# One-level Strassen for the query and key projections: seven block products, weight sums on GpSimd, additions on VectorE

## The reference

```python
h = rms_norm(x, pre_norm_gain)            # 256 x 1024
proj = h @ w_in                           # q: 3 x 512 columns, k: 3 x 512 columns, v, rwkv, gates
...
logits = einsum('bdhnqc,bdhnkc->bdhnqk', qb, kb) * scale + bias      # scale = 1 / 8
```

## Time and profile before

| | |
|---|---|
| time, median of 3 runs | 1834.88 us (1834.88 to 1836.4) |
| the profiled execution, own time | 1837.94 us |
| its span, first to last instruction | 1835.8 us |
| PE busy | 1375.2 us (75%) |
| DVE busy | 435.8 us (24%) |
| ACT busy | 144.8 us (8%) |
| POOL busy | 36.4 us (2%), 53 instructions |
| mean granted TensorE clock | 0.855 |
| DMA | 629.55 MB, mean 343 GB/s |

### The profile page before, as it was taken

How to read it: one execution, slowest core, us unless ns; L and a number is a source line. 1 busy time by engine, 2 the same in 40 slices (tenths; PEclk the granted TensorE clock), 3 DMA queues, 4 the chain that set the end, 5 groups by cost and what they waited for, 6 DMA issues and landing times.

```text
span 1835.8 us, 21606 instructions
## 1 busy us (share of the span) xinstructions
PE 1375.2 (75%) x10034; PEld 769.3 (42%) x10034; DVE 435.8 (24%) x671; ACT 144.8 (8%) x316; POOL 36.4 (2%) x53
## 2 busy tenths in 40 slices
PE   9999999999999865756666674756656575766655
PEld 7888577858665321313222231322322131322311
DVE  3543224357653211010102101010210101021012
ACT  3200012113131000000000000000000000000001
POOL 1001010000000000000000000000000000000000
PEclk9999999999999978777787787878787787778788
DMA  7324363333389999999999999999999999999995
GB/s 256 138 94 144 110 224 117 112 127 111 124 328 392 430 435 429 432 432 428 436 430 431 432 431 430 427 434 432 427 434 432 430 433 426 430 434 431 431 428 238
DMA packets 54909, 629.55 MB, mean 343 GB/s; under 512 B 3546, under 2 KB 4741, under 8 KB 37412
## 3 DMA queue, kind: packets, MB, share of 16 engines
q1 hardware_dynamic: 51952, 620.02, 80.4%
q0 software_dynamic: 2448, 7.82, 1.5%
q10 hardware_dynamic: 420, 0.34, 0.1%
HBM read 627.05 MB, written 1.11 MB: 342 GB/s over the span
## 4 chain that ended last, share of the span: by engine, by line
PE 53%; DMA 33%; another core or an unknown queue 8%; DVE 4%; ACT 1%; issue 1%; POOL 0%; POOLq 0%; DVEq 0%; SPq 0%; ACTq 0%
DMA arena<-in_w_up 25%; PE psum L1453 12%; PE psum L890 12%; PE psum L1503 6%; DMA arena<-in_w_gate 5%; PE psum L1442 4%; PE psum L1232 3%; DMA arena<-in_w_down 3%; PE psum L1162 2%; PE psum L1321 2%; PE psum L893 2%; PE psum L969 1%; DVE arena L2109 1%; PE psum L896 1%; PE psum L1136 1%
## 5 line engine op out<-in xcount | busy, mean ns | idle before, releaser
L1453 PE MATMUL psum<-arena 128*32 128x352 f32 x4096 | 418.8, 573 | 335.3 <-DMA arena<-in_w_up 207.3
L1453 PEld LDWEIGHTS psum<-arena 128*32 128x32 f32 x4096 | 149.7, 133 | 604.4 <-issue 246.2
L1503 PE MATMUL psum<-arena 128*32 128x512 f32 x1408 | 230.7, 729 | 48.0 <-DMA arena<-in_w_down 48.0
L890 PE MATMUL psum<-arena 128*128 128x256 f32 x976 | 221.6, 383 | 1.3 <-ACT arena L601 0.7
L890 PEld LDWEIGHTS psum<-arena 128*128 128x128 f32 x976 | 181.9, 189 | 29.8 <-issue 2.2
L2102 DVE TENSOR_SCALAR arena<-arena 128x704 f32<-128x704 f32 x16 | 8.4, 528 | 639.6 <-ACT arena L836 639.5
L1503 PEld LDWEIGHTS psum<-arena 128*32 128x32 f32 x1408 | 67.1, 128 | 198.2 <-issue 122.9
L2109 DVE TENSOR_TENSOR arena<-psum,arena 128x704 f32<-128x704 f32 x16 | 21.5, 1345 | 318.2 <-PE psum L1453 318.2
L1442 PEld LDWEIGHTS psum<-arena 128*128 128x128 f32 x512 | 93.1, 285 | 1.5 <-issue 1.1
L1442 PE MATMUL psum<-arena 128*128 128x32 f32 x512 | 93.4, 357 | 0.2 <-DVE arena L2066 0.2
L839 ACT ACTIVATE arena<-psum 128x1024 f32<-128x1024 f32 x15 | 15.4, 1024 | 775.1 <-PE psum L1503 775.1
(11 more groups left out here) (373 smaller groups left out, 970.0 us busy)
## 6 DMA issues: line engine op xcount, KB each, us to landing
arena<-in_w_gate SPq DMA_DIRECT2D x22, 5632.0 KB, 53.8
arena<-in_w_up SPq DMA_DIRECT2D x21, 5632.0 KB, 52.1
arena<-in_w_down SPq DMA_DIRECT2D x19, 5632.0 KB, 54.6
arena<-in_w_up SPq DMA_DIRECT2D x21, 2816.0 KB, 48.1
arena<-in_w_down SPq DMA_DIRECT2D x20, 2816.0 KB, 54.1
arena<-in_w_gate SPq DMA_DIRECT2D x20, 2816.0 KB, 50.2
arena<-in_w_in SPq DMA_DIRECT2D x24, 2048.0 KB, 8.7
arena<-in_w_down SPq DMA_DIRECT2D x11, 1408.0 KB, 50.4
```

What stands on the lines that cost most here:

```text
L890: last = mm(o, block_of(blk)[:, k, c * P:c * P + P], rhs[:, k, :], start=(k == 0), stop=(k == KC - 1))
L1453: last = mm(psum[32 * j:32 * j + CAP, b + n, 0:HALFQ], XC[:, k, :], region(o, HALFQ), start=(k == 0), stop=(k == KC - 1))
L1503: last = mm(psum[32 * g:32 * g + CAP, gate + 1 - n, :], HT[:, i, :], region(spot(pos), 512), start=(i < 4), stop=(i >= FPP - 4))
```

## The change

The two halves of the 1024 inputs, the two halves of a block's 512 output columns and the two halves of the 256 tokens make each projection a 2 x 2 by 2 x 2 block product. The usual way takes eight block products, Winograd's form of Strassen's method takes seven, with sums of weight blocks, sums of token blocks and sums of the results.

- PE: a block's four tiles are now A, B, C and D. A, B and C hold two block products each (left and right half of the PSUM bank), D holds one. One block product is 8 matmuls (2 x 4) of a 128 x 128 weight tile with 128 columns, 16 instructions (L971 of the new kernel).
- POOL: four sums of 512 columns over the tokens (`T1` to `T4`), once for `hT` and once for `hR`, and per block four sums of 1024 columns: `S1`, `S2`, and two in place in the weight block, the last of them after product A has read it. Each waits for the one before. 32 instructions in all. They stand before the bias DMAs in POOL's queue.
- ACT copies out only the first half of A; DVE does all other read-outs as additions or subtractions in `halves_added(j)`: one instruction of 256 columns from PSUM for A, two for B, three for C, one for D.
- `S1`, `S2`, `T1` to `T4` take up buffer `wb[1]`, so that q0 to k2 use two weight buffers, by the table `SLOTS`.
- The factor 0.125 moves into DVE's addition of the bias to the logits.
- Tile 19 moves behind the first group of Gram products, and DVE's read-out of tile 13 stands ahead of `token_shift(2)`.

```diff
+        S1, S2 = region(4096, 4, 256), region(5120, 4, 256)
+        T1, T2, T3, T4 = (region(6144 + 512 * i, 4, P) for i in range(4))
+        SLOTS = (0, 2, 1, 0, 2, 0, 2, 0, 2, 0, 2, 1, 0, 2)
+        def tenant_before(n):
+            if blocks[n][0] == "v1":
+                return "k2"
+            return next((blocks[i][0] for i in reversed(range(n)) if slot_of(i) == slot_of(n)), None)
...
-        tiles += [(f"q{i}", c, hT, qT[:, 4 * i + c, :], 0.125) for i in range(3) for c in range(4)]
-        tiles += [(f"k{i}", c, hR, kT[:, 4 * i + c, :], 1.0) for i in range(3) for c in range(4)]
+        tiles += [(f"q{i}", c, hT, qT[:, 4 * i:4 * i + 4, :], 1.0) for i in range(3) for c in "ABCD"]
+        tiles += [(f"k{i}", c, hR, kT[:, 4 * i:4 * i + 4, :], 1.0) for i in range(3) for c in "ABCD"]
...
+            def summed(dst, x, y, op):
+                nc.gpsimd.tensor_tensor(dst, x, y, op).then_inc(S["w_sums"], 1)
+                sums[0] += 1
+                pool.wait_ge(S["w_sums"], sums[0])
+            def token_sums(h):
+                summed(T1, h[:, 0:4, P:T], h[:, 0:4, 0:P], ALU.subtract)
+                summed(T2, h[:, 4:KC, P:T], T1, ALU.subtract)
+                summed(T3, h[:, 4:KC, P:T], h[:, 0:4, P:T], ALU.subtract)
+                summed(T4, T2, h[:, 4:KC, 0:P], ALU.subtract)
+            def weight_sums(name):
+                w, j = block_of(name), first_of(name)
+                weights_in(pool, name)
+                if j > Q_TILE:
+                    pool.wait_ge(S["proj_ready"], j - 2)
+                summed(S1, w[:, 0:4, T:2 * T], w[:, 4:KC, T:2 * T], ALU.add)
+                summed(S2, S1, w[:, 0:4, 0:T], ALU.subtract)
+                summed(w[:, 0:4, T:2 * T], w[:, 0:4, 0:T], w[:, 0:4, T:2 * T], ALU.subtract)
+                if name == "k0":
+                    pool.wait_ge(S["proj_ready"], j)
+                    token_sums(hR)
+                pool.wait_ge(S["proj_ready"], j + 1)
+                summed(w[:, 4:KC, 0:T], w[:, 4:KC, 0:T], S2, ALU.subtract)
+            pool.wait_ge(S["proj_ready"], first_of("rkv2"))
+            token_sums(hT)
+            for name in SEVEN:
+                weight_sums(name)
             pool.wait_ge(S["T1_mm"], 5)
...
+            def block_product(j, slot, w, h):
+                for f in range(2):
+                    o = psum[:, bank_of(j), slot * T + f * P:slot * T + f * P + P]
+                    for k in range(4):
+                        last = mm(o, w[:, k, f * P:f * P + P], h[:, k, :], start=(k == 0), stop=(k == 3))
+                return last
+            def seven_products(j):
+                blk, c, h = tiles[j][0:3]
+                w = block_of(blk)
+                if c in "BC":
+                    pe.wait_ge(S["w_sums"], sums_at(j))
+                if c == "A":
+                    block_product(j, 0, w[:, 0:4, 0:T], h[:, 0:4, 0:P])
+                    last = block_product(j, 1, w[:, 4:KC, 0:T], h[:, 4:KC, 0:P])
+                elif c == "B":
+                    block_product(j, 0, S2, T2)
+                    last = block_product(j, 1, S1, T1)
+                elif c == "C":
+                    block_product(j, 0, w[:, 0:4, T:2 * T], T3)
+                    last = block_product(j, 1, w[:, 4:KC, 0:T], h[:, 4:KC, P:T])
+                else:
+                    last = block_product(j, 0, w[:, 4:KC, T:2 * T], T4)
+                last.then_inc(S["proj_ready"], 1)
...
                     before = [i for i in range(j) if bank_of(i) == bank_of(j)]
-                    if before:
-                        pe.wait_ge(S["proj_evac"], before[-1] + 1)
+                    if before and seven(before[-1]):
+                        pe.wait_ge(S["half_read"], halves(before[-1]))
...
+            def halves_added(j):
+                c = tiles[j][1]
+                left, right = part(j, 0), part(j, 1)
+                c11, c12, c21, c22 = (quarter(j, i, t) for i in range(2) for t in range(2))
+                if c == "A":
+                    dve.wait_ge(S["proj_evac"], evacs(j))
+                    last = V.tensor_tensor(c11, right, c12, ALU.add)
+                else:
+                    dve.wait_ge(S["proj_ready"], j + 1)
+                    dve.wait_ge(S["half_read"], halves(j - 1))
+                if c == "B":
+                    link(V.tensor_tensor(c12, left, c12, ALU.add))
+                    last = V.tensor_tensor(c22, right, c12, ALU.add)
+                elif c == "C":
+                    link(V.tensor_tensor(c21, left, c12, ALU.add))
+                    link(V.tensor_tensor(c12, right, c22, ALU.add))
+                    last = V.tensor_tensor(c22, left, c22, ALU.add)
+                elif c == "D":
+                    last = V.tensor_tensor(c21, c21, left, ALU.subtract)
+                last.then_inc(S["half_read"], 1)
...
-            token_shift(2).then_inc(S["v_shift"], 1)
+            halves_added(13)
+            token_shift(2).then_inc(S["ab_ready"], 1)
+            for j in (14, 15, 16):
+                halves_added(j)
             dve.wait_ge(S["bonus_mm"], 1)
```

More of the change, by code:

```diff
@@ L429, in program, with seven, evacs, halves @@
         assert (Q_TILE, V_TILE, Z_TILE, G_TILE, NT) == (13, 37, 43, 51, 67)
+        def seven(j):
+            return Q_TILE <= j < V_TILE
+        def evacs(j):
+            return sum(not seven(i) or tiles[i][1] == "A" for i in range(j + 1))
+        def halves(j):
+            return sum(seven(i) for i in range(j + 1))
+        def quarter(j, i, t):
+            blk, c, rhs, dst, scale = tiles[j]
+            x = dst[:, 2 * i:2 * i + 2, :]
+            if blk == "k0":
+                return x[:, :, t * P:t * P + P]
+            return x.rearrange("p f (r j) -> p f r j", r=4)[:, :, :, 32 * t:32 * t + 32]
+        def part(j, i):
+            x = psum[:, bank_of(j), i * T:i * T + T]
+            if tiles[j][0] == "k0":
+                return x.rearrange("p (f t) -> p f t", f=2)
+            return x.rearrange("p (f j r) -> p f r j", f=2, r=4)
         def bank_of(j):
@@ L439, in program, with first_of, sums_at @@
         tiles2 += [(f"at{i}", c) for c in range(4) for i in (0, 1)]
+        SEVEN = ("q0", "q1", "q2", "k0", "k1", "k2")
+        def first_of(name):
+            return min(j for j, t in enumerate(tiles) if t[0] == name)
+        def sums_at(j):
+            blk, c = tiles[j][0:2]
+            n = SEVEN.index(blk)
+            if blk == "k0":
+                return 23 if c == "B" else 24
+            return 4 + 4 * n + (4 if n > 3 else 0) + (2 if c == "B" else 4)
         def bank2_of(j):
@@ L481, in second_out @@
             def second_out(n, name, src):
-                count, value = released[blocks[n - NB][0]]
+                count, value = released[tenant_before(n)]
                 sp.wait_ge(count, value)
-                sp.dma_start(wb[(n + 1) % NB], src).then_inc(wload[(n + 1) % NB], 16)
+                sp.dma_start(wb[slot_of(n)], src).then_inc(wload[slot_of(n)], 16)
             def expert_rows(n):
@@ L526, in _ @@
             pool.dma_start(rows, A["rows"][a:b].partition_broadcast(P)).then_inc(S["rows_in"], 16)
+            sums = [0]
+            def summed(dst, x, y, op):
[24 more added lines that the diff above has]
+                weight_sums(name)
             pool.wait_ge(S["T1_mm"], 5)
@@ L603, in evac @@
             def evac(j):
+                if seven(j) and tiles[j][1] != "A":
+                    return
                 act.wait_ge(S["proj_ready"], j + 1)
                 blk, c, rhs, dst, scale = tiles[j]
+                if seven(j):
+                    act.activation(quarter(j, 0, 1), part(j, 0), ACT.Copy).then_inc(S["proj_evac"], 1)
+                    return
                 src = psum[:, bank_of(j), 0:T if rhs is not None else 512]
@@ L1135, in up_rwkv @@
                 for f in range(FT):
-                    last = mm(psum[:, j % 4, 0:T], wb_up[(number["upr"] + 1) % NB][:, f, j * P:j * P + P], orT[:, f, :], start=(f == 0), stop=(f == FT - 1))
+                    last = mm(psum[:, j % 4, 0:T], wb_up[slot_of(number["upr"])][:, f, j * P:j * P + P], orT[:, f, :], start=(f == 0), stop=(f == FT - 1))
                 last.then_inc(S["up_mm"], 1)
@@ L1149, in _ @@
                 for f in range(FT):
-                    last = mm(psum[:, j % 4, 0:T], wb_up[(number["upa"] + 1) % NB][:, f, j * P:j * P + P], oaT[:, f, :], start=(f == 0), stop=(f == FT - 1))
+                    last = mm(psum[:, j % 4, 0:T], wb_up[slot_of(number["upa"])][:, f, j * P:j * P + P], oaT[:, f, :], start=(f == 0), stop=(f == FT - 1))
                 last.then_inc(S["up_mm"], 1)
```

63 lines of the change are left out of this document (41 added, 22 removed).

## The result

| | before | after |
|---|---|---|
| time, median of 5 runs each | 1834.88 us (1834.56 to 1836.4) | 1844.29 us (1843.63 to 1844.69) |
| span of the profiled execution | 1835.8 us | 1842.5 us |
| POOL busy | 36.4 us | 107.3 us |
| DVE busy | 435.8 us | 471.0 us |

The ratio is 1.0050, 95% interval 1.0035 to 1.0064. The kernel became 9.4 us slower; the forecast was 6.9 us faster, and the time lies above the range. The case that came is the second rival, and it came dearer than I priced it.

A forecast was written before the change was run, and what follows sets the result against it. PE was taken to bound the projection stage, with expert-weight DMA behind it shifting 1 to 1. A gain of 8.1 us less 1.2 us contention gave 6.9: 1834.9 to 1828 us, own range 1826 to 1831, overall 1826 to 1842.

The forecast's parts named there:

- the second rival: Before tile C (15), POOL and DVE hold each other in turn: 10.1 us idle PE, 5.4 us slower, 1840 us; chance 0.24.
- most of the sums slip under the reciprocal and in between: In DVE's preparation, POOL's sums mostly run beside the reciprocal and in gaps, costing 1.2 us.
- 10.6 us of lateness: At tile 13's read-out, DVE's delay under full exclusion from POOL's sums, with 6.5 us hidden under the reciprocal.
- The price of 1.9 us a sum: On POOL, a sum of 1024 columns takes 1.9 us, taken from a copy of 2048 columns.
- 3.4 for the clock: Behind PE's idle before tile C, work lost to a lower clock over three 4 us stretches: 3.4 us.
- The first rival: Before tile C, DVE holds POOL and sums come late: 1.0 us gain, 1834 us; chance 0.28.
- The gain of 8.1 us: In PE's six q and k blocks, 112 instructions at 111.7 ns replace 64 at 216.7 ns: 1.36 us saved per block.
- The third rival: In the projections, the 128-column pace is 114 ns or worse: 1829.6 us and up; little weight, within the forecast's range.
- The solve: DVE's added read-outs during the solve are covered by PE's other work; no cost counted.
- The weights with two buffers: Loads for q1, v1 and v2 start later but arrive in time: no cost, 3 us to spare at worst.
- the later bias DMAs: Bias DMAs, held back about 10 us behind the last block's sums, are wanted only beyond 243 us: no cost.
- 0.3 to 0.5 us to spare: In block q0, DVE's read-outs of A and B free their banks just before PE's tiles C and D need them.

The follow-up runs named there:

- experiments 2 and 3: Changed kernel with each POOL sum replaced: first by a memset that writes and reads nothing, 1827.31 us; then by a copy of its first operand, 1831.4 us.
- experiment 5: Changed kernel with the token sums and q0's first three sums run ahead of DVE's preparation, in memory of their own: 1836.18 us.
- early_late: Changed kernel with token sums and q0's first three sums early, in memory of their own, and q1's sums waiting until DVE has done token_shift(2): 1830.2 us.

## Why the prediction was wrong

**The step that failed** is "I forecast that most of the sums slip under the reciprocal and in between, and put 1.2 us on it". DVE's read-out came 15.7 us late, because the sums and the preparation's two-operand instructions shut each other out; in place of 1.2 us the term cost 15.3 us of idle PE and 2.7 us of restart and clock, 18.0 in all. I rested the milder view on the row at 546 us, where a DVE instruction of 0.36 us ran in full inside a POOL instruction. Its few columns were named as a doubt, and yet I let it outweigh what spoke for the hold. It also has one SBUF operand, while nearly all of DVE's preparation but the reciprocal has two; and its own kind, 256 columns at L1723, was held too once POOL's sum was long (four of them 3.11 us, 1.14 alone). Most of what POOL did could not slip under the reciprocal: seven sums began at 46.5, the reciprocal at 58.1, and POOL then had 2.2 us left to do; for the rest of the reciprocal it waited for product A. The place and the direction were those of the second rival, which had a chance of 0.24; it deserved most of it.

The Trainium skill, "SBUF — State Buffer", "Who interferes with whom", had the rule and I did not follow it: whichever of the two starts first has the shared port pair for the whole instruction. The trace agrees: 1.22 us became 3.36 beside a sum of some 2.3 us. It names two VectorE inputs as held only against a GpSimd instruction that reads SBUF, and experiments 2 and 3 agree: unheld beside writes, 1.94 us beside a copy.

**The second rival's size.** It had 10.6 us of lateness, 17.1 of sums less 6.5 hidden. Sums that ran with little or nothing of DVE beside them took 5.24 us for four of 512 and 6.84 for three of 1024 columns (experiment 5), and the in-place one of q1 2.35 (changed kernel, 96.21 us); up to the read-out that makes 5.24 + 2 x 6.84 + 2.35 = 21.3 us, 4.2 more, and 21.3 - 15.7 = 5.6 were hidden, 0.9 less: 10.6 + 5.1 = 15.7. The price of 1.9 us a sum was thus a sixth too low; 6.84 / 3 = 2.28 was right. The Trainium skill, "GPSIMD Engine Reference", "Performance versus the Vector engine", gives 4497 ns for an addition of 2048 columns; half of it, an estimate of 2.25 us for 1024, agrees with the trace's 2.28. That the hidden part came close to my 6.5 us is chance. I had it all under the reciprocal, and only 2.2 us were there; the other 3.4 come mostly from this, that a sum held DVE for less than it takes: 2.0 to 2.1 of 2.28 us, and 0.8 to 1.1 of 1.31 us for 512 columns. Restart and clock cost 2.7 us, where I had 3.4 for the clock.

**The first rival** did not come: PE waited for DVE, and no wait of PE for one of POOL's sums stands in the trace. POOL was held too (seven sums in 13.76 us that take 12.1 alone), but its sums for B were done at 60.3, 5.3 us ahead of need.

**What was right.** The gain of 8.1 us: with 111.7 ns per instruction the six blocks gave 8.1 us at the first expert load, and 8.6 us of time, without sums. The third rival's 114 ns did not show. The solve lost nothing: from the bonus product to the first expert load 422.5 us passed with the sums and 422.6 without them, and from 95 to 250 us PE waited for nothing. POOL's sums there met mostly DVE's read-outs from PSUM, which run on; one two-operand product was held (L1777, 118.55 us, 3.40 us in place of 1.23), and PE did not need it sooner. Rows of DVE, and POOL's beside them, in the changed kernel:

```profile
106.10 3.08 DVE L1752 TENSOR_TENSOR arena<-psum,arena 128x512 f32<-128x512 f32 x5 [1.18 <-PE psum L1077]
110.33 0.42 DVE L1692 TENSOR_TENSOR arena<-psum,arena 128x256 f32<-128x256 f32 x1 [1.15 <-PE psum L971]
```

```profile
104.17 7.22 POOL L587 TENSOR_TENSOR arena<-arena 128x1024 f32<-128x1024 f32 x3 [5.61 <-PE psum L971]
```

The weights with two buffers were in time, the later bias DMAs cost nothing, and the rate behind 575 us stayed at 430 GB/s. And the margin was named: "0.3 to 0.5 us to spare" before C and D. In a place with so little room the one open cost decides the sign, so it should have set the forecast.

## What to carry to other kernels

Before work goes to GpSimd, list what VectorE does in the same microseconds: an instruction with two SBUF operands, or a fast one-operand one, waits for nearly the whole length of a GpSimd instruction that reads SBUF (here 1.22 us became 3.3), so in these traces such work was free only beside PSUM read-outs, the reciprocal and idle time. Put the instruction that gives back a buffer, or releases PE, ahead of whatever can be held, and start the GpSimd work as early as its inputs are there: both together turned +9.4 us into -8.0. When a place has half a microsecond to spare, a cost that the trace leaves open there must be taken at its dear end.

## What the runs showed of the hardware that I had not expected

- The hold goes both ways and by whole instructions: three sums and three products came in strict turn, at 3.3 us for a pair of 2.1 and 1.2.
- A one-operand DVE instruction that is fast alone (1024 columns in 0.69 us) is held too: 2.72 us beside additions, 1.41 beside copies, and 1.26 beside pure writes, which left two-operand products at 1.22. The reciprocal, also with one SBUF operand but 6.55 us long, was held by none of the three.
- What PE loses behind an idle stretch does not grow with the stretch: 2.7 us after 15.3 idle, 1.8 after 10.8 and 2.1 after 2.8 with 128-column products behind, but 4.4 after 6.9 us where the bonus product and the transposes follow. In early_late 2.15 us of idle time cost only 0.4, and the clock stayed at 1.00. Each figure is from one trace; what decides it was not tested, and stays open.
